# Weight tiles loaded ahead of their stage, and the later stages of a hybrid DeltaNet/attention layer as one block

## What is computed

```
def merge_branches(y_dn, y_at, gates, w_branch_dn, w_branch_attn, w_out):
    g_dn, g_at = jnp.split(gates, 2, axis=-1)
    merged = jax.nn.sigmoid(g_dn) * (y_dn @ w_branch_dn) + jax.nn.sigmoid(g_at) * (y_at @ w_branch_attn)
    return merged @ w_out
...
    x = x + g_a_x * merge_branches(y_dn_x, y_at_x, mg_x, w_branch_dn, w_branch_attn, w_out)
    x = x + g_f_x * conv_ffn(modulate(rms_norm(x, norm_ffn), sh_f_x, sc_f_x), ffn_up, ffn_conv, ffn_conv_b, ffn_down)
```

## Time and profile before

| | |
|---|---|
| median of 3 runs | 3016.35 us (3010.81 to 3019.44) |
| profiled execution | 3021.34 us, span 3019.4 us |
| PE matmul | 2665.3 us busy, 88% of the span, 16326 instructions |
| DVE, ACT, POOL busy | 1424.4, 828.5, 881.4 us |
| granted PE clock, mean | 0.931 of full speed |
| DMA | 175.41 MB, 58 GB/s on average |

### The profile page before, as it was taken

How to read it: one execution, slowest core, us unless ns; L and a number is a source line. 1 busy time by engine, 2 the same in 40 slices (tenths; PEclk the granted TensorE clock), 3 DMA queues, 4 the chain that set the end, 5 groups by cost and what they waited for, 6 DMA issues and landing times. The chain is left out here.

```text
span 3019.4 us, 45024 instructions
## 1 busy us (share of the span) xinstructions
PE 2665.3 (88%) x16326; PEld 2180.8 (72%) x16326; DVE 1424.4 (47%) x2403; ACT 828.5 (27%) x1532; POOL 881.4 (29%) x609
## 2 busy tenths in 40 slices
PE   3898998798898989898998988797859999997999
PEld 2666776686777878786777776586638888886877
DVE  5672664202456565665746566321134555555242
ACT  3221443101243443526243433100131112212010
POOL 2332776232232231313132220232203333332111
PEclk8999999899798989899998989798879999998999
DMA  5101111311000000001010000332221111112433
GB/s 212 58 28 56 70 77 70 132 63 63 14 16 22 15 25 13 30 8 37 1 36 22 15 8 1 132 111 92 96 90 54 46 47 49 49 49 71 130 114 102
DMA packets 49495, 175.41 MB, mean 58 GB/s; under 512 B 4688, under 2 KB 13136, under 8 KB 47952
## 3 DMA queue, kind: packets, MB, share of 16 engines
q1 hardware_dynamic: 47056, 169.19, 16.2%
q10 hardware_dynamic: 2304, 4.20, 0.4%
HBM read 148.20 MB, written 25.17 MB: 57 GB/s over the span
## 5 line engine op out<-in xcount | busy, mean ns | idle before, releaser
L193 PE MATMUL ps_up<-h_hi,up_w_hi 128*128 128x512 f32 x704 | 274.7, 390 | 37.3 <-POOL up_w_lo L183 37.3
L194 PE MATMUL ps_up<-h_lo,up_w_hi 128*128 128x512 f32 x704 | 274.3, 390 | 0.0
L195 PE MATMUL ps_up<-h_hi,up_w_lo 128*128 128x512 f32 x704 | 274.3, 390 | 0.0
L2175 DVE TENSOR_SCALAR ffn_u<-ffn_pad,vectors 128x1024 f32<-128x1024 f32 x44 | 105.3, 2393 | 230.6 <-ACT ffn_pad L2155 230.6
L1305 PE MATMUL dn_bank<-h_hi,dn_w_hi 128*128 128x512 f32 (+1 forms) x512 | 193.2, 377 | 12.6 <-POOL dn_w_lo L183 12.6
L1305 PE MATMUL dn_bank<-h_lo,dn_w_hi 128*128 128x512 f32 (+1 forms) x512 | 193.0, 377 | 0.0
L1305 PE MATMUL dn_bank<-h_hi,dn_w_lo 128*128 128x512 f32 (+1 forms) x512 | 192.9, 377 | 0.0
L193 PEld LDWEIGHTS ps_up<-h_hi,up_w_hi 128*128 128x128 f32 x704 | 132.5, 188 | 65.8 <-issue 38.1
L2244 PE MATMUL ps_down<-act_hi,down_w_hi 128*128 128x512 f32 x352 | 138.8, 394 | 24.1 <-DVE act_lo L2283 24.1
L1682 DVE SCALAR_TENSOR_TENSOR conv_out<-conv_in,head_taps,conv_out 128x1284 f32<-128x1284 f32 (+1 forms) x96 | 154.5, 1610 | 0.4
L176 POOL CAST up_w_hi<-up_w_raw 128x1024 fp32r<-128x1024 f32 x44 | 45.7, 1039 | 371.3 <-PE ps_up L195 311.3
(11 more groups left out here) (359 smaller groups left out, 7024.1 us busy)
## 6 DMA issues: line engine op xcount, KB each, us to landing
up_w_raw<-in_w_up SPq DMA_DIRECT2D x44, 512.0 KB, 3.3
down_w_raw<-in_w_down SPq DMA_DIRECT2D x32, 704.0 KB, 4.1
late_w_ada<-in_w_ada SPq DMA_DIRECT2D x8, 2048.0 KB, 9.8
dn_w_raw<-in_w_dn SPq DMA_DIRECT2D x32, 512.0 KB, 4.0
w_ada<-in_w_ada SPq DMA_DIRECT2D x8, 1024.0 KB, 12.0
at_w_raw<-in_w_mg_at SPq DMA_DIRECT2D x16, 512.0 KB, 4.2
dnm_w_raw<-in_w_mg_dn SPq DMA_DIRECT2D x16, 512.0 KB, 5.4
x_in<-in_xT SPq DMA_DIRECT2D x8, 640.0 KB, 8.9
```

What stands on the lines that cost most here:

```text
L193: pe.matmul(out, self.hi[j][:, k, :], xh, start=(k == 0), stop=False)
L194: pe.matmul(out, self.hi[j][:, k, :], xl, start=False, stop=False)
L195: mm = pe.matmul(out, self.lo[j][:, k, :], xh, start=False, stop=(k == self.kt - 1))
L2175: ins = dve.tensor_scalar(u[:, s, :], src, tap(0), vec[:, bass.ds(m + s * FT + V_CONVB, 1)], ALU.mult, ALU.add)
```

## The change

1. The first two weight tiles of the attention merge, of the delta net, of the delta merge and of the down projection are loaded, and all but the last split, in the stage in front (`ahead` makes the ring's semaphores early; `ring_at` places all these rings at the same place at the end of SBUF). A clearing of semaphores is added between window attention and its merge, between the delta net and the late stage, and between the late stage and down.
2. Both merges run all eight gate tiles first, keep the eight sigmoids in SBUF, and then run the eight branch tiles.
3. Delta merge, out, norm and up are one block, `late_stage`. The merged sum is not stored: DVE and ACT split it where it lies. Out runs over the eight w_out tiles for the first 512 tokens and again for the others, so each tile is loaded and split twice. The squares are summed over slices by DVE, and PE sums over partitions once per half. The norm of the first half runs beside out's last products; the norm of the second half beside the first halves of the first two up tiles; the second halves of these tiles then go slice by slice.
4. In down, the conversions of the second half wait slice by slice for a use of the first (`act_free`), and two splits of DVE come between its first subtractions.

```diff
 window_attention, gpsimd and sync:
                 rounds(pool, body)
+                for j in range(2):
+                    at_w.split_tile(pool, j, 0, j, freed=False)
...
                 rounds(sp, body)
+                ada_step.wait(sp, HEADS // 2 * 8)
+                for j in range(2):
+                    at_w.load(sp, j, d["w_mg_at"][:, 2 * j], j, first=True)
                 for jj in range(2):
                     sp.wait_ge(y_stored[jj], HEADS // 2 * 16 + 16)
...
+def at_merge(core, d):
+            def _(sp):
+                for i in range(2, 2 * LINES):
+                    w.load(sp, i, d["w_mg_at"][:, source(i)], i % 2)
+                    if i - 2 < KT:
+                        sp.dma_start(y_raw[:, i - 2, :], core.y_dram[:, i - 2, :]).then_inc(y_in[i - 2], 16)
+                    m = i - LINES - 2
+                    if m >= 0:
+                        made.wait(sp, m + 1)
+                        sp.dma_start(core.merged_dram[:, m, :], sig[:, m, :]).then_inc(stored, 16)
+                for j in range(2):
+                    sp.wait_ge(w.split, 2 * LINES - 1 + j)
+                    dn_w.load(sp, j, d["w_dn"][:, j], j, first=True)
...
+            def _(pool):
+                for i in range(2, 2 * LINES):
+                    w.split_tile(pool, i, i // 2, i % 2)
+                for j in range(2):
+                    w.used.wait(pool, 2 * LINES - 1 + j)
+                    dn_w.split_tile(pool, j, 0, j, freed=False)
...
 attention:
         window_attention(core, d, a)
-    merge_stage(core, "at", core.y_dram, d["w_mg_at"], core.merged_dram)
+    core.retire_semaphores()
+    core.dn_w = ahead(core, "dn", at=ring_at(core))
+    at_merge(core, d)
...
 delta_net, last head, gpsimd and sync:
+            else:
+                for j in range(2):
+                    grp.wait(pool, h * NPROJ + (TILE_END[T_Q], TILE_END[T_GATE])[j])
+                    late_w.split_tile(pool, j, 0, j, freed=False)
...
+                else:
+                    for j in range(2):
+                        sp.wait_ge(w.split, HEADS * 4 - 1 + j)
+                        late_w.load(sp, j, d["w_mg_dn"][:, 2 * j], j, first=True)
...
+def late_stage(core, d, act_t):
+            def _(sp):
...
+                for q in range(2 * KT):
+                    i = LATE_OUT + 2 + q
+                    w.load(sp, i, source(i), i % 2)
+                    x1_made.wait(sp, q - 1)
+                    sp.dma_start(x_in[:, q % 2, :], d["xT"][:, q % KT, half(q // KT)]).then_inc(x_res_in[q % 2], 16)
+                x1_made.wait(sp, 2 * KT)
+                sp.dma_start(core.x1_dram, x1[:, :, :]).then_inc(x1_stored, 16)
+                down_w.load(sp, 1, d["w_down"][:, 0, KP:2 * KP], 1, first=True)
...
+            def _(pe):
...
+                for q in range(2 * KT):
+                    i = LATE_OUT + q
+                    pe.wait_ge(w.split, i + 1)
+                    x1_made.wait(pe, q - 1)
+                    mm = w.product(pe, x1_place(q), i % 2, m_hi, m_lo, q // KT * HALF, HALF,
+                                   parts=m_lo_made if q == 0 else None)
+                    mm.then_inc(w.used.sem, 1)
+                    if q == KT + 1:
+                        squares(0)
+                for t in range(2):
+                    pe.wait_ge(w.split, LATE_UP + t + 1)
+                    h_lo_made.wait(pe, KT)
+                    x1_made.wait(pe, 2 * KT - 1)
+                    up_half(t, 0)
+                    if t == 0:
+                        squares(1)
+                for t in range(2):
+                    for k in range(KT):
+                        h_lo_made.wait(pe, KT + k + 1)
...
+            def _(dve):
...
+                def residual(q):
+                    t, b = q % KT, q // KT
+                    w.used.wait(dve, LATE_OUT + q + 1)
+                    dve.wait_ge(x_res_in[q % 2], q // 2 * 16 + 16)
+                    dve.scalar_tensor_tensor(out=x1[:, t, half(b)], in0=x1_place(q), scalar=core.gate_mix[:, t:t + 1],
+                                             in1=x_in[:, q % 2, :], op0=ALU.mult, op1=ALU.add).then_inc(x1_made.sem, 1)
+                    sq_made.wait(dve, q + 1)
...
+                        dve.tensor_tensor(acc, acc, sq[:, q % 2, :], ALU.add).then_inc(acc_made.sem, 1)
+                for q in range(KT + 2):
+                    residual(q)
+                root(0)
+                for q in range(KT + 2, 2 * KT):
+                    residual(q)
+                    for k in steps_of(q):
+                        scaled(0, k)
+                    for k in steps_of(q):
+                        low(0, k)
+                root(1)
+                scaled(1, 0)
+                for k in range(KT):
+                    if k + 1 < KT:
+                        scaled(1, k + 1)
+                    low(1, k)
+                dve.wait_ge(x1_stored, 16)
...
 ffn_down, scalar and vector:
                 for half in range(2):
-                    if half == 1:
-                        w.used.wait(act, 2 * KT)
                     for k in range(FT):
+                        if half == 1 and k % KP == KP - 1:
+                            w.used.wait(act, 2 * KT - 1 + k // KP)
+                        elif half == 1:
+                            act.wait_ge(act_free, k - k // KP + 1)
                         act.activation(hi_t[:, k, :], act_t[:, half, k, :], ACT.Copy).then_inc(hi_ready, 1)
...
-                for part in range(2):
-                    w.split_rest(dve, part, part)
                 for half in range(2):
                     for k in range(FT):
+                        if half == 0 and k in (2, 5):
+                            w.split_rest(dve, k // 5, k // 5)
```

More of the change, by code:

```diff
@@ L27 @@
 FT = D_FF // P
+KP = FT // 2
 TAPS = 5
@@ L1946, in prologue @@
             def prologue():
[L1947 to L1948 removed]
+                for n in range(2, 4):
+                    w.load(sp, n, d["w_dn"][:, n], n % 2)
             def body(h, fill):
@@ new lines, in _, with squares @@
+                for m in range(KT):
+                    pe.wait_ge(w.split, LATE_BRANCH + m + 1)
+                    gated_made.wait(pe, m - 1)
+                    for b in range(2):
+                        mm = w.product(pe, ps[2 + m % 2][:, half(b)], m % 2, y_hi, y_lo, b * HALF, HALF,
+                                       parts=y_lo_made if m == 0 and b == 0 else None)
+                    mm.then_inc(w.used.sem, 1)
+                def squares(b):
+                    acc_made.wait(pe, (b + 1) * KT)
+                    gated_made.wait(pe, KT)
+                    pe.matmul(ps[3][:, half(b)], mats[:, C_ONE, :], rstd[:, half(b)], start=True, stop=True).then_inc(ss_done, 1)
@@ new lines, in _, with up_tile @@
+                pe.wait_ge(std_made, 2)
+                def up_tile(t, place):
+                    pe.wait_ge(w.split, t + LATE_UP + 1)
+                    copied.wait(pe, t - 3)
+                    for b in range(2):
+                        mm = w.product(pe, ps[place][:, half(b)], place % 2, h_hi, h_lo, b * HALF, HALF)
+                    mm.then_inc(w.used.sem, 1)
+                for t in (2, 3):
+                    up_tile(t, t)
+                with pe.Fori(1, FT // 2) as i:
+                    for place in range(4):
+                        up_tile(i * 4 + place, place)
@@ new lines, in root, with scaled @@
+                def root(b):
+                    dve.wait_ge(std_made, b + 1)
+                    dve.reciprocal(rstd[:, half(b)], rstd[:, half(b)]).then_inc(rstd_made, 1)
+                    dve.wait_ge(rstd_made, b + 1)
+                def scaled(b, k):
+                    h_lo_made.wait(dve, b * KT + k - 1)
+                    dve.scalar_tensor_tensor(out=tmp[:, k % 2, :], in0=x1[:, k, half(b)], scalar=core.scale_ffn[:, k:k + 1],
+                                             in1=rstd[:, half(b)], op0=ALU.mult, op1=ALU.mult).then_inc(xs_made, 1)
@@ new lines, in low @@
+                def low(b, k):
+                    h_hi_made.wait(dve, b * KT + k + 1)
+                    dve.scalar_tensor_tensor(out=h_lo[:, k, half(b)], in0=tmp[:, k % 2, :], scalar=core.mod[:, 3 * KT + k, 0:1],
+                                             in1=h_hi[:, k, half(b)].bitcast(F32), op0=ALU.add,
+                                             op1=ALU.subtract).then_inc(h_lo_made.sem, 1)
+                for q in range(KT + 2):
+                    residual(q)
+                root(0)
@@ L2221, in body @@
                             "p a n -> p (a n)")).then_inc(x_loaded[j], 16)
-                    tiles(sp, half, body)
+                    whole = half == 1
+                    body(0, 0, 0)
+                    whole = True
+                    body(1, 0, 1)
+                    with sp.Fori(1, KT // 2) as i:
+                        for j in range(2):
+                            body(i * 2 + j, i, j)
             @block.gpsimd
@@ L2251, in _ @@
                         first = False
```

(5 more changed lines are left out.)

562 lines of the change are left out of this document (242 added, 320 removed).

## The result

The changed kernel takes 2941.01 us (median of 4 runs, 2937.82 to 2943.87) beside 3017.89 us of the kernel before on the same chip (4 runs, 3010.81 to 3023.54): a ratio of 0.974, 95% interval 0.9725 to 0.9755. It is faster, as predicted, but by 77 us and not by the forecast 104; the forecast was 2912 and the range ended at 2934.

A forecast was written before the change was run, and what follows sets the result against it. PE, busy 88% of the span, sets the end, so gains lie at seams where it stands or runs slow. Terms 6.2 + 6.3 + 14.5 + 71.4 + 5.5 + 0 = 103.9 us gave 2912.4 us; range 2897 to 2934.

The forecast's parts named there:

- attention merge: Attention's last matmul to merge end: loads not early, gap 13.5 us, gates first hide y's split; gain 6.2 us.
- delta net, its gap included: Seam before the delta net: early loads and splits cut the gap from 12.6 to 6.3 us; gain 6.3 us.
- delta merge: Tiles split in the last delta head, PE starts 4.9 us after its last matmul; 195.8 to 181.3 us, gain 14.5.
- merge to up's second tile: Last delta merge product to end of up's second tile: 198.7 us before, 127.3 after, gain 71.4 us.
- rest of up: Up after its second tile: the prediction gave it no term, so a gain of 0.
- down, its gap included: Seam before down: 18.0 us becomes 12.5 with first tiles ready, despite added semaphore clearing; gain 5.5 us.
- 0.2265 us each: Matmul time read in up's and down's long stretches (2106 in 477.00 us), giving 5.44 or 10.87 us per tile.
- 2.5 us of low clock: Cost added behind up's second halves, for the low clock left by PE's pauses there.
- between the halves: Down's two halves: conversions stay queued behind the first half's last output DMA; gain 0, at best some 1 us.
- No sharing: Rival: VectorE's scaled and low steps don't wait for GpSimd; 6.3 us less or more, about 2905 us; chance 0.17.
- Pool starved: Rival: GpSimd loses the SBUF side to VectorE, splits in out take 6.5 us; about 2925 us; chance 0.19.
- The seams don't shorten: Rival: barriers, not weights, set the seams, so only merged in SBUF and out to up count; about 2941 us; chance 0.05.

The follow-up runs named there:

- 6: Changed kernel with the attention merge's first two weight loads issued ahead of the wait for attention's last y store: 2929.23 us, ratio 0.9689.
- 7: Changed kernel with first loads and splits of attention merge, delta net, delta merge and down put back to their own stage's head: 2955.44 us, ratio 0.9774.
- run 8: Changed kernel with GpSimd splitting only one column of the weight tiles in out's last six products and up's first two: 2940.84 us, one run.
- run 9: Changed kernel, down's second-half conversions ahead of ScalarE's output DMA and VectorE's last result: 2943.05 us; second try, eleven subtractions ahead, eleven behind: 2935.8 us.

## Why the prediction was off

By its own terms, gain in us from one stage's last matmul to the next's, in profiled executions:

| term | predicted | changed kernel | ring 32 bytes lower |
|---|---|---|---|
| up to attention's last matmul | 0 | 5.4 | 3.7 |
| attention merge | 6.2 | −0.5 | 4.7 |
| delta net, its gap included | 6.3 | 3.3 | 9.3 |
| delta merge | 14.5 | 9.7 | 14.3 |
| merge to up's second tile | 71.4 | 73.2 | 73.6 |
| rest of up | 0 | −13.5 | 0.0 |
| down, its gap included | 5.5 | 4.8 | 4.1 |
| sum | 103.9 | 82.4 | 109.7 |

**The step that failed** is the first paragraph's "0.2265 us each", used in every term for a tile of 5.44 or 10.87 us, and its silent partner, that the rest of up costs the same as before, though the change puts these rings at another place. That pitch was read where weights and tokens had the same remainder, and the change gives it up. 4032 matmuls by 0.0067 us (470.40 less 456.90, over 2016) are 27.0 us: 5.1 in each merge, 3.2 in out and up's first tiles, 13.5 in the rest of up. With the ring 32 bytes lower the time is 2911.61 us, by ratio 3.6% under before, where the forecast was 2912. Part of that closeness is luck: 4.3 us inside the delta net, whose ring had been at remainder 64, and 3.7 ahead of attention's last matmul were not in the sum. (That matmul ended anywhere from 524.1 to 529.6 us in nine profiled executions with the first projections' ring at 224, so the changed kernel's 5.4 may be scatter alone; in four with the ring at 192 it ended between 519.9 and 526.0, so part of the 3.7 is the pitch of the first projections.)

**The attention merge.** Loads not early: right, shown by 6 and 7; gap 14.5 for 13.5. Its gain was to come from the gates in front of the branches, and with the pitch restored it does (4.7).

**The delta net and the delta merge.** Gaps 7.6 for 6.3 and 5.2 for 4.9; no wait for y. Right in mechanism, 1.3 us short at the first, where PE waited for nothing that the trace names.

**Merge to up.** Right to 2 us, by errors that cancel. The first out product waited 2.25 us for 2.5. Out's last products and the first up tile waited 2.7 us for 6.3: the mechanism is shown by run 8, but I let each GpSimd operation hold VectorE for its whole length, where steps that had begun before it were not held (the pair of 1.42) and others met only its end. Up's second halves came at 1.45 us a slice for 1.4. The 2.5 us of low clock behind them were not paid (clock 1.00), and the slower pitch took 3.2.

**Down.** 13.3 for 12.5; and between the halves nothing moved, as written, 6.0 us. What I gave as the reason, a DMA queued in front of the conversions, was half of it: run 9 shows that VectorE's order and GpSimd's cast decide too.

**The rivals.** "No sharing" falls by run 8, "Pool starved" did not happen in out: no product there waited for a split. It did in run 9, where the casts took 11.32 us. "The seams don't shorten" named 2941, the measured time, but not its cause: the gaps did shorten. No rival had a cost inside PE's own matmuls.

## What to carry to other kernels

A table that changes its place is a change of its own: a pitch may be taken from one stage for another only if both tables lie alike, so read the median of a matmul in each stage before any table is moved, and for float32r matmuls of 512 columns put weights and tokens at the same remainder of 256 bytes. Where the same instruction has three lengths in one trace at one clock (389, 393 and 396 ns), explain them before you predict. A load moved ahead of a stage's end helps when its splits are done by about the time of the last store; at the attention merge the gap was 12.4 us with the loads at the head of the stage, 14.5 with them behind that store and 5.2 in front of it.

## What the runs showed of the hardware

The float32r matmuls of 512 columns have a pitch of 0.2266 us (456.90 over 2016) when weights and moving tokens have the same byte remainder of 256, and 0.2333 us (470.40 over 2016) in the pairing 224 with 192, 2.9% more, at full granted clock and with the same count of instructions. It follows neither the region of the memory nor a multiple of 64 or 128 bytes.

At 256 columns equal remainders are not faster. The first projections also have 240 matmuls of that width, in which the weight table is the moving side; by tile, in the changed kernel (224 with 192) and with the ring 32 bytes lower (192 with 192):

```profile
L555 PE MATMUL ps_rot<-aproj_w_hi,h_hi x80: 277/280/683, 257.9 to 286.0; 128*128 128x256 f32 x80
```

```profile
L555 PE MATMUL ps_rot<-aproj_w_hi,h_hi x80: 280/283/682, 256.6 to 285.4; 128*128 128x256 f32 x80
```

The run of them takes 28.1 us with different remainders and 28.8 with the same one. The delta net's 384 matmuls of 256 columns, with the tokens moving, last 289 or 290 ns in the mean at 224 with 192 and 291 at 192 with 192. Whether it is the width, the moving side or the form of these matmuls that takes the gain away, whether other types show either effect, and what in the chip makes it, was not tried and stays open. The Trainium skill's page "SBUF — State Buffer", section "Operand start alignment", gives a multiple of the element size as the rule for where an operand may start, and says that this is about legality and that its runs timed nothing; all places used here keep that rule, and the 3% lie beyond it.
